# A two-part transformer block in split float32: operands at other byte offsets

## What is computed

```python
# part one, each layer (first_block)
h = rms_norm(x);  z = h @ w_in + b_in             # 1024 -> 2824 columns
x = x + concat(mlstm(z), hgrn2(z), window_attention(z)) @ w_out
h = rms_norm(x);  x = x + relu(h @ w_up)**2 @ w_down          # 4096 inner features
x = x + ... (p @ w_ple_proj), gated by h @ w_ple_gate         # "PLE", 256 -> 1024
# part two, each layer (second_block)
h = rmsnorm(x) * (1 + scale1) + shift1
x = x + gate1 * mixer_layer(h, w_in, w_out, ...)  # three kinds of attention
h = rmsnorm(x) * (1 + scale2) + shift2
u, g = split(h @ w_up)                            # 2816 inner features each
x = x + gate2 * ((silu(causal_conv(g)) * u) @ w_down)
# at the end rmsnorm(x)
```

## Time and profile before

| | us |
|---|---|
| median of 3 runs | 2967.53 (2966.63 to 2968.41) |
| the profiled execution, whole | 2967.89 |
| its span in the profile | 2966.0 |
| TensorE busy (matmuls / weight loads) | 2815.3 / 2340.2 |
| VectorE / ScalarE / GpSimd busy | 1615.2 / 1128.1 / 193.0 |

### The profile page before, as it was taken

One profiled execution on the slowest core, in us unless ns is written; L12 is line 12 of the kernel. 1 busy time (PEld: TensorE's weight loads), 2 busy tenths in 40 slices (PEclk: granted clock), 3 DMA queues, 4 the chain that ended last, 5 costly groups with the idle time before them and its releaser, 6 DMA issues. The chain is left out here.

```text
span 2966.0 us, 37027 instructions
## 1 busy us (share of the span) xinstructions
PE 2815.3 (95%) x14756; PEld 2340.2 (79%) x14756; DVE 1615.2 (54%) x2705; ACT 1128.1 (38%) x1712; POOL 193.0 (7%) x192
## 2 busy tenths in 40 slices
PE   6999899999899899999989999899998999899998
PEld 5877788888788677888878878788887887788887
DVE  5755566655765648555576434543544534454443
ACT  6445322223554433322354444432323344332232
POOL 1310100002121110000120000100000000100001
PEclk9987999999899699999999999999998999999999
DMA  4210154343221014444422111223222210122322
GB/s 158 72 43 29 54 187 179 144 169 114 102 79 58 15 61 161 155 164 149 170 84 90 57 34 40 83 85 110 93 76 103 72 42 31 57 100 79 114 82 68
DMA packets 42978, 278.80 MB, mean 94 GB/s; under 512 B 6072, under 2 KB 6456, under 8 KB 11704
## 3 DMA queue, kind: packets, MB, share of 16 engines
q1 hardware_dynamic: 42808, 276.44, 26.4%
HBM read 274.33 MB, written 2.10 MB: 93 GB/s over the span
## 5 line engine op out<-in xcount | busy, mean ns | idle before, releaser
L306 DVE TENSOR_TENSOR low_panels<-raw_panels,high_panels 128x2048 fp32r<-128x2048 f32 (+3 forms) x218 | 469.6, 2154 | 337.9 <-ACT high_panels L293 337.8
L293 ACT ACTIVATE high_panels<-raw_panels 128x2048 fp32r<-128x2048 f32 (+3 forms) x218 | 392.6, 1802 | 460.4 <-PE bank L1549 149.4
L424 PE MATMUL bank<-mlp_h_high,high_panels 128*128 128x512 f32 x1152 | 451.8, 392 | 0.0
L424 PE MATMUL bank<-mlp_h_high,low_panels 128*128 128x512 f32 x1152 | 450.6, 391 | 0.0
L424 PE MATMUL bank<-mlp_h_low,high_panels 128*128 128x512 f32 x1152 | 449.2, 390 | 0.0
L424 PEld LDWEIGHTS bank<-mlp_h_high,low_panels 128*128 128x128 f32 x1152 | 216.5, 188 | 45.7
L424 PEld LDWEIGHTS bank<-mlp_h_low,high_panels 128*128 128x128 f32 x1152 | 216.4, 188 | 45.6
L424 PEld LDWEIGHTS bank<-mlp_h_high,high_panels 128*128 128x128 f32 x1152 | 216.5, 188 | 44.4
L449 PE MATMUL bank<-high_panels,h_high 128*128 128x256 f32 x704 | 206.5, 293 | 0.5 <-ACT values_and_ones L2061 0.5
L424 PE MATMUL bank<-h_high,high_panels 128*128 128x512 f32 x496 | 203.5, 410 | 0.2
L1549 PE MATMUL bank<-mlp_hid_high,high_panels 128*128 128x512 f32 x512 | 203.4, 397 | 0.0
(11 more groups left out here) (346 smaller groups left out, 5111.4 us busy)
## 6 DMA issues: line engine op xcount, KB each, us to landing
raw_panels<-in_w SPq DMA_DIRECT2D x236, 1024.0 KB, 4.8
raw_panels<-in_w SPq DMA_DIRECT2D x16, 384.0 KB, 3.1
raw_panels<-in_w SPq DMA_DIRECT2D x4, 960.0 KB, 4.6
raw_panels<-in_w SPq DMA_DIRECT2D x4, 768.0 KB, 4.1
row<-in_row SPq DMA_DIRECT2D x2, 1220.0 KB, 6.1
x<-in_xT SPq DMA_DIRECT2D x2, 1024.0 KB, 6.0
raw_panels<-in_w SPq DMA_DIRECT2D x4, 512.0 KB, 3.4
mix<-in_rope SPq DMA_DIRECT2D x2, 1024.0 KB, 6.1
```

The source lines that it names most:

```text
L293: self.nc.scalar.activation(self.g.high[:, j % SPLIT, 0:raw.shape[1]], raw, ACT.Copy).then_inc(self.high_ready, 1)
L306: self.nc.vector.tensor_tensor(self.g.low[:, j % SPLIT, 0:w], raw, self.g.high[:, j % SPLIT, 0:w].bitcast(F32), ALU.subtract).then_inc(sel ...
L424: ins = nc.tensor.matmul(bank[:, :], w[a][:, k, c0:c0 + P], rhs[b][:, k0 + k, :], start=first and k == 0 and j == 0, stop=last and k == kt ...
```

## The change

Unused tensors of 16 or 24 columns (64 or 96 bytes) are allocated ahead of certain operands. Nothing is written to them or read from them. The instructions, their order, sizes and waits are the same on all engines; only addresses differ.

```diff
 mlp_one
-        hh, hl = sb("mlp1_h_high", [P, DC, S], F32R), sb("mlp1_h_low", [P, DC, S], F32R)
-        uh, ul = sb("mlp1_hid_high", [P, DC, S], F32R), sb("mlp1_hid_low", [P, DC, S], F32R)
+        hh = sb("mlp1_h_high", [P, DC, S], F32R)
+        sb("to_line_h_low", [P, 16])
+        hl = sb("mlp1_h_low", [P, DC, S], F32R)
+        sb("to_line_hid_high", [P, 24])
+        uh = sb("mlp1_hid_high", [P, DC, S], F32R)
+        sb("to_line_hid_low", [P, 16])
+        ul = sb("mlp1_hid_low", [P, DC, S], F32R)
 layer_two
+        sb("to_line_h2_high", [P, 16])
         hh = sb("h2_high", [P, DC, S], F32R)
+        sb("to_line_h2_low", [P, 16])
         hl = sb("h2_low", [P, DC, S], F32R)
 mlp_two
-        hh, hl = sb("mlp2_h_high", [P, DC, S], F32R), sb("mlp2_h_low", [P, DC, S], F32R)
-        uh, ul = sb("mlp2_hid_high", [P, HALF2, S], F32R), sb("mlp2_hid_low", [P, HALF2, S], F32R)
+        sb("to_line_mlp2_high", [P, 16])
+        hh = sb("mlp2_h_high", [P, DC, S], F32R)
+        sb("to_line_mlp2_low", [P, 16])
+        hl = sb("mlp2_h_low", [P, DC, S], F32R)
+        sb("to_line_mlp2_hid_high", [P, 24])
+        uh = sb("mlp2_hid_high", [P, HALF2, S], F32R)
+        sb("to_line_mlp2_hid_low", [P, 16])
+        ul = sb("mlp2_hid_low", [P, HALF2, S], F32R)
 program
         kc = sb("kc", [P, K_WIDTH])
+        sb("to_line_all", [P, 24])
         g.x = sb("x", [P, DC, S])
         g.raw = sb("raw_panels", [P, RAW, PANEL])
         g.high = sb("high_panels", [P, SPLIT, PANEL], F32R)
+        sb("to_line_low", [P, 16])
         g.low = sb("low_panels", [P, SPLIT, PANEL], F32R)
```

## The result

The change makes the kernel slower: 3003.04 us as the median of 4 runs (2999.18 to 3005.38) beside 2967.08 for the kernel before on the same chip, a ratio of 1.0121 (95% interval 1.0106 to 1.0137). The profiled execution has a span of 3001.3 us against 2966.0, 35.3 us more, at the same mean granted clock (0.962).

A forecast was written before the change was run, and what follows sets the result against it. TensorE's own pace, read from matmul starts, was taken to bound the dense stages. Savings of 17.1 + 13.4 + 9.4 = 39.9 us gave 2967.9 - 39.9 = 2928.0, as a median 2927.6 us; range 2893 to 2990.

The forecast's parts named there:

- the mixers' share: 512-column and token rows in the mixers: 18.9 us saved, half counted, 9.4, since VectorE and ScalarE chains would take over.
- Step (a): h and panels in dense products: rows starting on a 64-byte boundary save time, to 220.0 ns; 39.9 us less.
- My bound at the worst end: 512-column h rows: at worst the pace of the slowest run seen with the lower extra, 233.1 ns.
- Step (b): The MLPs' inner rows, 32 bytes off the weights: 0 taken, bounds -20.7 to +13.8 us.
- Step (c): All other moved tensors: no cost; VectorE's 2154 ns panel split stays hidden behind 10.9 us of matmuls.
- Rival A: Dense products: only the distance between moving row and weights counts, not where they begin; 2963 to 2969 us, chance 0.22.
- Rival B: Dense products: rows alternating between two offsets don't settle; +33.8 us, 3001 us, chance 0.23, a third of it mild.
- point of decision: All 512-column rows of part two: a mean pace of some 229 ns would decide for alternating rows not settling.
- argument against: Against unsettled alternating rows: a run settles within eight steps everywhere in the trace.
- The tokens of part one: 256-column token rows in part one: distance 64 to mostly 0, 1344 x 6.3 ns, half counted, +4.2 us.

The follow-up runs named there:

- all0: The kernel before with both panel tensors and every h, p and inner row at offset 0 modulo 128: 2981.76 us, ratio 1.0042.
- all32: The kernel before with both panel tensors and every h, p and inner row at offset 32 modulo 128: 2981.20 us, ratio 1.0049.
- the map: Six variants of the kernel before, each stage's operands placed at its own distance to the weights; one execution each, 2966.85 to 2996.88 us.
- after_h_by_128: The changed kernel with h of the MLPs and part two's mixer moved 384 bytes, distance 0 again, halves and panels still 64 apart: 2992.03 us, 1.0086.
- map4: The kernel before with low panels 64 bytes from the high ones and activations at various distances per stage: 2996.37 us, one execution.
- before_mlp2_by_128: The kernel before with h and inner rows of part two's MLPs moved 128 bytes, distance 0 to 128: 2987.63 us, ratio 1.0075.
- map2: The kernel before with panels at 160 modulo 512, each stage's activations at another distance, both halves alike: 2994.71 us, one execution.
- part1_distance0: The kernel before with a 192-byte pad moving part one's MLP and PLE from distance 64 to 0: 2964.44 us over 11 runs, ratio 0.9994.

## Why the prediction was wrong

**What bounds the kernel, and how it is read: right.** No other engine's busy time has moved by more than 2 us and no wait has come in; where TensorE is never idle, in the MLPs, the difference is in the distance of its starts. It holds at the upper clock alone, as the forecast had read from the earlier trace rows. Of the mixers' share I had counted half; 10.3 of 15.5 us came through in the profiled execution, but the mixers vary by as much with the clock, so that the half is neither confirmed nor refuted.

**Step (a) failed**, the 64-byte boundary: 220.0 ns taken for every h row, 232.2 measured in part two's MLP, 232.04 in part one's, 233.3 in PLE. It came from extras that looked like pieces of 6.67 ns. all0 and all32 show that it makes no difference whether a row begins at 0 or at 32 modulo 64, and the map has values that no whole number of pieces gives (228.9, 231.1, 234.2). The step was -39.9 us; the same rows cost +33.9 (42 us less the 8.0 of the inner rows), about 29 with the mixers at 10.3. My bound at the worst end, 233.1, was the right end to take; PLE lies even past it. A smaller slip: four of the counts leave out the 96 rows each of `project_as_ready` (L438), so 1920, 2016, 720 and 1104 should be 2016, 2112, 816 and 1200.

**Step (b)**, the inner rows, 0 taken: +3.3 and +4.7 us by their paces, within its bounds (-20.7 to +13.8). The distance of 32 that the trace didn't have is one of the poor ones (233.3 alone; 231.1 with the halves 64 apart).

**Step (c)** held: 2154 ns and no wait on `low_panels` that counts.

**Rival A** had the right kind of rule and the wrong numbers. It looked to the distance between the two operands and not to where they begin, as all0 and all32 bear out; but I took it modulo 128, because that was the table I had made. Modulo 256 the pads change part two's h from 0 to 128 and part one's from 64 to 128, and by the map this alone gives 232.3 to 233.3, no gain and no draw. And it took 0 with 0, then 64 with 64, for as good as 0 throughout, which after_h_by_128 and map4 refute.

**Rival B** gave 3001 us, 2 below the result, and its point of decision, a mean pace of 229 ns in part two, was passed (232.2). As a mechanism it is half shown: rows that alternate between two offsets do cost 4.4 ns even at the best distance, and in after the steps do stay uneven (228 to 237 ns). But at the distance of 128, which B didn't have, they are as uneven without any alternation (228 to 242 in before_mlp2_by_128), and this alone would have cost as much. That B's sum comes so near is therefore in part luck. Its argument against, that a run settles within eight steps everywhere in the trace, was wrong as well: the 32 steps of the earlier trace rows stay at 233.1 ns. The tokens of part one, +4.2 in it, are 7.5 us by count.

The range ended at 2990 because I left out most of B. Rows 7, 233.1 ns at the offsets that gave 228.9 elsewhere, and rows 8 showed losses as large as those that came; no stretch of the trace had rows of 512 columns at a pace under 226.7 ns. And the addresses modulo 256 and 512 were to be had before the run.

**What stays open.** Why these distances are good (0, 240, and 64) and others bad, why 0 is bad by token, and why the two halves of one stage of after_h_by_128 run at 231.1 and 232.2 ns, or those of map2 at 232.4 and 233.3: the runs give the numbers, not the cause. No version beats before; part1_distance0 is level with it.

## What to carry to other kernels

Where TensorE is the bound, read its pace from the starts of consecutive matmuls, stage by stage, and compare it with the addresses of the two operands that are read together, modulo 256 and not only modulo the size of a supposed line. For a split product in float32r keep the high and low tensors at the same offset modulo 256, and a moving row of 512 columns at a distance of 0 from the weights (64 costs 1%, most others 2 to 3%). For 256 columns with the roles exchanged the best distance was 192, up to 5% better than 0; since swapping the roles turns the sign, one place of h can't be best for both. Stages that change by a few us have to be compared at the same clock. A pad ahead of one tensor shifts all that follow it, so every pad needs the whole table of distances again, in every stage.

## What was not expected of the hardware

- The pace of 512-column float32r matmuls depends on the relative addresses of the moving row and the next weights: 226.7 to 237.7 ns at equal work, 113.3 to 121.2 (after, over 46 steps) for 256 columns. The Trainium skill, "SBUF — State Buffer", section "Who interferes with whom", has independent read ports and a TensorE that waits for nobody. The trace of all0 doesn't fit it: 226.7 and 232.3 ns in one kernel at equal work.
- At 1.2 GHz nothing of this is seen: 426 ns in after, as the 426.7 before, where the same rows have 232.2 and 226.7 at 2.4 GHz.
- The period is 256 bytes, and 4 bytes are enough: 226.7 ns at distance 0, 237.7 at 4.
- Equal distances don't suffice. With both operands 64 bytes further on from product to product and back, 231.1 ns replace 226.7.
- The same offsets can settle at different paces: 231.1 and 232.2 ns in the two halves of one stage of after_h_by_128, 232.4 and 233.3 in map2, 120.9 and 117.8 by token in after.
